# A decoder step on one core: GpSimd adds the squares of the output projection's first twelve results, and TensorE sums the first half one fill sooner

## The reference

```python
y = jnp.einsum('bte,ed->btd', o, w_o)          # output projection
def rms_norm(x, g):
    xf = x.astype(jnp.float32)
    y = xf * lax.rsqrt(jnp.mean(xf * xf, axis=-1, keepdims=True) + EPS)
    return (y * g.astype(jnp.float32)).astype(x.dtype)
hp = hp + rms_norm(yp, g[1])
hp = hp + rms_norm(sq_relu_mlp(rms_norm(hp, g[2]), mlp_w1[i], mlp_w2[i]), g[3])
```

## Time and profile before

| | us |
|---|---|
| median of 3 runs | 1491.09 |
| their range | 1486.6 to 1492.05 |
| profiled execution | 1489.39 |
| its span in the trace | 1487.0 |
| TensorE busy | 1445.9 |
| DVE busy | 895.9 |
| ACT busy | 421.9 |
| GpSimd busy | 354.4 |

### The profile page before, as it was taken

How to read it: one execution, slowest core, us unless ns; L and a number is a source line. 1 busy time by engine, 2 the same in 40 slices (tenths; PEclk the granted TensorE clock), 3 DMA queues, 4 the chain that set the end, 5 groups by cost and what they waited for, 6 DMA issues and landing times. The chain is left out here.

```text
span 1487.0 us, 25888 instructions
## 1 busy us (share of the span) xinstructions
PE 1445.9 (97%) x9729; PEld 1206.7 (81%) x9729; DVE 895.9 (60%) x1957; ACT 421.9 (28%) x1065; POOL 354.4 (24%) x463
## 2 busy tenths in 40 slices
PE   8999999999999899999999999999999999999998
PEld 7877999655557788888888889688888888888888
DVE  2755444888454985664767735666585556776513
ACT  3011343888421533334200002443431111000012
POOL 0000300477340379990320033370000000000000
PEclk9999999999999999999999999999999999999999
DMA  8346670411685624464344321712313131322201
GB/s 276 106 137 152 191 210 28 129 51 58 211 293 115 240 100 161 139 221 167 116 130 129 100 65 52 289 49 80 109 57 113 58 113 57 113 85 86 85 29 58
DMA packets 144429, 184.34 MB, mean 124 GB/s; under 512 B 31298, under 2 KB 103690, under 8 KB 143282
## 3 DMA queue, kind: packets, MB, share of 16 engines
q1 hardware_dynamic: 141938, 176.41, 36.5%
q0 software_dynamic: 2368, 6.30, 1.2%
HBM read 163.42 MB, written 29.69 MB: 130 GB/s over the span
## 5 line engine op out<-in xcount | busy, mean ns | idle before, releaser
L2842 POOL TENSOR_SCALAR att_p<-att_p,att_tot,gates 128x128 f32<-128x128 f32 (+3 forms) x128 | 79.1, 631 | 45.5 <-DVE att_tot L2764 44.8
L1062 PE MATMUL psum<-l_up_t,l_w_sums 128*128 128x260 f32 x336 | 78.2, 382 | 0.0
L1062 PE MATMUL psum<-xT,l_w 128*128 128x260 f32 x320 | 74.0, 383 | 1.6 <-PEq L113 1.6
L305 PE MATMUL psum<-xT,l_w 128*128 128x260 f32 x320 | 72.6, 388 | 1.8 <-PEq L113 1.8
L2364 PE MATMUL psum<-cmp_xt,cmp_w 64*128 64x256 f32 (+1 forms) x640 | 72.2, 362 | 0.3 <-DVE cmp_xt L2285 0.3
L1062 PEld LDWEIGHTS psum<-l_up_t,l_w_sums 128*128 128x128 f32 x336 | 63.8, 190 | 9.8
L305 PEld LDWEIGHTS psum<-xT,l_w 128*128 128x128 f32 x320 | 61.8, 194 | 11.9 <-issue 2.2
L2815 ACT ACTIVATE att_p<-att_p,att_low 128x128 f32<-128x128 f32 (+3 forms) x128 | 70.4, 554 | 3.1 <-DVE att_low L2755 3.1
L1062 PEld LDWEIGHTS psum<-xT,l_w 128*128 128x128 f32 x320 | 60.7, 190 | 11.1 <-issue 1.8
L1356 ACT ACTIVATE l_hidden<-l_tmp 128x260 f32<-128x260 f32 x64 | 26.4, 420 | 146.8 <-DVE l_tmp L1576 146.8
L2755 DVE CUSTOM_DVE_ANT_0 att_p<-psum,causal 128x128 f32<-128x128 f32 (+3 forms) x128 | 55.8, 487 | 18.9 <-PE psum L2587 17.9
(11 more groups left out here) (628 smaller groups left out, 3200.8 us busy)
## 6 DMA issues: line engine op xcount, KB each, us to landing
l_w<-in_mlp_w SPq DMA_DIRECT2D x16, 2048.0 KB, 7.7
l_w<-in_mlp_w SPq DMA_DIRECT2D x32, 1024.0 KB, 5.3
sa_rows<-in_cache_kv_sel SPq DMA_DIRECT2D x68, 128.0 KB, 2.5
proj_w<-in_nsa_w_in SPq DMA_DIRECT2D x4, 2048.0 KB, 10.1
cmp_raw<-in_cache_kv_cmp SPq DMA_DIRECT2D x24, 256.0 KB, 3.0
xT<-in_cache_kv_cmp SPq DMA_DIRECT2D x24, 256.0 KB, 3.0
hT<-in_cache_kv_cmp SPq DMA_DIRECT2D x16, 256.0 KB, 3.1
l_w<-in_nsa_w_o SPq DMA_DIRECT2D x2, 2048.0 KB, 13.0
```

Source lines behind the costliest of these rows:

```text
L305: mm = nc.tensor.matmul(ps[:, n % 8, 0:HALF], w[s][:, k, m * P:(m + 1) * P], src[:, kk, cols(h)], start=(kk == 0), stop=(kk == last))
L1062: mm = nc.tensor.matmul(ps[:, bank, 0:HALF], left(k), right(k), start=(fresh and k == 0), stop=(ends and k == KC - 1))
L2842: ve.tensor_scalar(pr[:, n % PR, par, at:at + w], pr[:, n % PR, par, at:at + w], tot[:, n % PR, u, par:par + 1], c.gates[:, i, gate:gate + ...
```

## The change

- TensorE: `sum_squares("mix", 0, 12)` stands behind fill 12 (`m == 0`) and no longer behind fill 13.
- ACT: the root of half 0 stands ahead of the copy and the square of fill 13.
- DVE: the powers run without a break; additions 0 to 11 are gone. Left are 12, ahead of the reciprocal of half 0, and 13, behind it, and 14 and 15 as before.
- GpSimd: `add_squares`, called by `tables.pool` behind the diagonal and ahead of the skip rows, does additions 0 to 11, each when its square is there, and waits until the twelfth is complete.

```diff
 @block.tensor
-                    if h == 1 and m == 1:
+                    if h == 1 and m == 0:
                         sum_squares("mix", 0, A_FILLS - 4)
 @block.scalar
-            for n in range(10, 14):
+            for n in range(10, 13):
                 keep_mix(n)
             root("mix", 0)
+            keep_mix(13)
             feed("mix", 0, 0, 3)
 @block.vector
-            def add_group(i):
-                for n in range(4 * i, 4 * i + 4):
-                    add_mix(n)
-
-            tables.dve_powers(dve, add_group)
-            for n in range(8, 14):
-                add_mix(n)
+            tables.dve_powers(dve)
+            add_mix(12)
             dve.wait_ge(c.h_back, 16)
             inverse("mix", 0)
+            add_mix(13)
             join("mix", 0, 0, 5)
 @block.gpsimd
+            def add_squares():
+                for n in range(A_FILLS - 4):
+                    h = n % 8 // 4
+                    pool.wait_ge(squared["mix"], n + 1)
+                    if n in (0, 4):
+                        nc.gpsimd.tensor_copy(acc[:, h], sq[:, n % 2]).then_inc(added["mix"], 1)
+                    else:
+                        pool.wait_ge(added["mix"], n)
+                        nc.gpsimd.tensor_add(acc[:, h], acc[:, h], sq[:, n % 2]).then_inc(added["mix"], 1)
+                pool.wait_ge(added["mix"], A_FILLS - 4)
 def pool(...)
             link(ve.tensor_copy(self.diag[at], c.ident[at, at]))
+        begin()
         pool.wait_ge(self.d_loaded, 16 * 4)
 def dve_powers(...)
-        between(0)
...
-        between(1)
```

More of the change, by code:

```diff
@@ L898, in _ @@
         def _(pool):
-            tables.pool(pool, lambda eng: eng.wait_ge(x_ready, 2 * KD), lambda eng: eng.wait_ge(up_done, 7 * PAIRS),
+            def add_squares():
[8 more added lines that the diff above has]
+                pool.wait_ge(added["mix"], A_FILLS - 4)
+            tables.pool(pool, add_squares, lambda eng: eng.wait_ge(x_ready, 2 * KD), lambda eng: eng.wait_ge(up_done, 7 * PAIRS),
                         lambda eng: eng.wait_ge(step_done, 7 * STEPS))
@@ L3591, in dve_k, with dve_powers @@
         ins.then_inc(self.k_kept, 1)
-    def dve_powers(self, dve, between):
+    def dve_powers(self, dve):
         c, ve = self.c, self.c.nc.vector
@@ L3685, in dve_powers, with pool @@
         dve.sem_inc(self.pw_ready, 1)
-    def pool(self, pool, mix_done, up_done, down_done):
+    def pool(self, pool, begin, mix_done, up_done, down_done):
         c, ve = self.c, self.c.nc.gpsimd
```

## The result

The changed kernel takes 1492.41 us (median of 20 runs, 1490.32 to 1496.14), the kernel before 1489.65 (20 runs beside them, 1486.6 to 1494.59): ratio 1.002, 95% interval 1.0012 to 1.0029. The change costs 2.8 us, by the interval 1.8 to 4.3. It was to bring 0.8.

The account below looks back on a forecast made before the run. TensorE, busy 97%, was taken as the bound, so only its waits or clock could count. 1489.39 us less 0.8 gave 1488.6; with the run median 1.7 above that execution, 1490.3 us, range 1485.5 to 1493.5.

Parts of the forecast that it names:

- GpSimd's additions: Additions 0 to 11 on GpSimd: 0.70 us each, 0.78 from start to start, the twelfth done at 494.0 us.
- The first wait goes: TensorE before the first sum of squares: its 3.46 us stall disappears, as the twelfth addition ends before fill 12.
- rival 3: DVE's joins of the first half: GpSimd's pushed-back chain ends too late, addition 15 at 515.6, time 1494.3 us; chance 0.22.
- One join per operation of GpSimd, at 1.1 to 1.4 us: DVE's joins beside GpSimd's b_bar products: one gets through per GpSimd operation, 1.1 to 1.4 us each, then 0.40 to 0.48.
- Rival 1: DVE's joins: two DVE operations per operation of GpSimd, gain 3.2 us, time 1487.9 us; chance 0.16.
- rival 2: DVE's joins: no hindrance by GpSimd, the full gain of 7.5 us, time 1483.6 us; chance 0.08.
- GpSimd's chain ends: GpSimd's 13.3 us of work queued behind the additions, up to the six products and sums, ends at about 507.4 us.
- The second sum: TensorE's second sum of squares starts at 513.3 us instead of 514.13, a gain of 0.8 us.
- One idle of 5.2 us instead of 5.84 in two: TensorE waits once, from 508.1 to 513.3 us before the second sum, instead of before both sums.
- Clock. "I take the same, so nothing in the sum": TensorE's low clock after the idle: costs the same 1.65 us as before, so adds 0 to the sum.
- twice as long (loss 1.7): Upper bound on the clock term: the low-clock stretch behind TensorE's idle doubles, a loss of 1.7 us.
- Nothing else changes behind the stage: TensorE behind the second sum: no new waits, since what it reads from DVE and ACT moves by the same amount.

Follow-up runs that it names:

- changed again: The changed kernel run once more, unaltered, for a second profile: 1494.58 us, ratio 1.0035 to the kernel before.
- padded: The changed kernel with 12 clears of 128x32 added on DVE behind the powers: 1493.15 us, ratio 1.0022 to the kernel before.
- sum moved alone: Kernel before with only the sum, root and addition 13 moved, DVE still doing all additions: 1491.57 us, ratio 1.0019.
- GpSimd adds alone: Only the additions moved to GpSimd; sum, root and addition 13 in the places of the kernel before: 1492.88 us, ratio 1.0022.
- again: The kernel before, unchanged but for one empty line ahead, timed once more: 1489.88 us, ratio 1.0003.
- with 12 more on GpSimd: The kernel before with 12 clears of 128x16 added on GpSimd where it waits for a DMA: 1489.13 us, ratio 0.9998.
- before, with both late edits: Kernel before with GpSimd's b_bar products behind the last x and TensorE's tables' products one or two pairs later: 1489.31 us, ratio 0.9995.
- the kernel kept busy: The changed kernel with 12 useless TensorE products ahead of the second sum: 1488.18 us, ratio 0.9994 to the kernel before.

## Why the prediction was wrong

Point by point:

- *GpSimd's additions*: 0.70 us taken, 0.73 measured; from start to start 0.78 taken, 0.88 measured for the seven in a row (6.00 us). The difference is idle time: 0.14 us before each, where the forecast took the 0.08 between two products of b_bar. Ahead of each addition the trace has a semaphore record of its own (L903, the wait for the addition before); between those products it has none. The 0.88 is the same beside DVE's last powers as behind them (from 492.8 on DVE is idle), so DVE is not the reason; it is DVE's small operations that take 0.62 us there instead of 0.19. The twelfth was complete at S + 32.9; predicted S + 32.35. In time for the sum: right.
- *The first wait goes*: right. *The root sooner*: ready at 499.51, S + 36.2 (predicted 497.8, which is the same S + 36.2).
- *Addition 12 beside L3715*: 2.03 us; the forecast gave it no price but named it in rival 3. It ended 0.3 us behind the root and made the reciprocal start 0.2 us behind it.
- *One join per operation of GpSimd, at 1.1 to 1.4 us*: right, 1.28, or 1.49 where GpSimd's own operation took 1.33. Rival 1 (two per operation) and rival 2 (no hindrance) fell.
- *GpSimd's chain ends* at 509.80, S + 46.5; predicted 507.4, S + 45.8. *The second sum* at S + 51.96; predicted S + 51.65. A schedule gain of 0.5 us for 0.8. Rival 3's chain never got late enough.
- *One idle of 5.2 us instead of 5.84 in two*: 5.70, in one piece: right.
- ***Clock. "I take the same, so nothing in the sum"***: this is the step that failed. The text had counted the idle's length and not its shape. One idle of 4.70 to 6.97 us was followed by 6.8 us of half clock in all five profiles that had one (changed, changed again, padded, sum moved alone, and GpSimd adds alone, which also stood 1.36 us shortly before), 2.4 to 2.9 us lost where it stands behind the second sum (2.7 in the mean of the changed kernel's three). The two shorter idles of the kernel before were followed by 3.4 us in all three profiles (before, again, and with 12 more on GpSimd), and in two of the three that stretch fell between the two sums, where the second wait took it up: 0, 0 and 1.7 lost, 0.6 in the mean. Waits of 0.44 and 2.70 us (before, with both late edits) also brought 3.4 us, and lost 1.7. The step should have read about +2.2 (0.8 to 2.9). The bound given, "twice as long (loss 1.7)", held the size of the profiled pair (1.1) and not that of the runs, since the 1.65 us of the earlier trace rows was itself the dear case of the kernel before. That the clock did it, and not the wait itself, is shown by the kernel kept busy: same second sum, the up projection 2.8 us sooner, and 3.9 us less in all.
- *Nothing else changes behind the stage*: also wrong, by 0.9 us in all seven profiles of kernels with GpSimd's additions; the cause is open.

Sum for the runs: -0.5 + 2.2 + 0.9 = 2.6 us; measured 2.8. (In the mean of three profiles of each, the second sum comes only 0.3 us sooner and the up projection 1.9 us later; with the 0.9 that is 2.8.) The predicted time, 1490.3, was built on a median of three runs that was 1.4 us above that of twenty (1491.09 to 1489.65), which hid part of the error: 1492.41 still fell within the range.

## What to carry to other kernels

Two short waits of the busiest engine are not the same as one long one of the same sum: price the granted clock behind each, and take it from several profiles, since one profile shows one draw. A stall that is gathered in one place can be filled with useless work as a test (and as a cheap cure: 2.8 us by the profiles here, 3.9 by the ratios). When a chain is pushed back, look for the next reader of its last result with the least time to spare; moving the chain paid only when that reader (the tables, 1.3 us to spare) was moved with it, and the change itself only together with both.

## What the runs showed of the hardware

- DVE and GpSimd beside one another take turns by whole instructions, but not always one for one. An addition of 128x260 on DVE: 0.43 us alone, 0.68 in the tail of one operation of GpSimd, 2.03 beside the four of L3715 (5.14 us), where it lasted beyond the ends of two of them (498.27 and 499.50), as the 3.13 us of the earlier trace rows (484.71 to 487.84) lasted beyond the ends of L3702 and of two L3708. GpSimd's own six took 1.12 to 1.34 us each meanwhile, beside the joins, and 1.06 to 1.34 before, beside the additions. The reciprocal, with one input, is 1.76 us beside GpSimd at 499.71 and 1.78 at 517.06 without it. The Trainium skill, SBUF — State Buffer, section "SBUF: two separate sides", calls the shared ports "an exclusive lock, not a bandwidth split"; these rows agree, in that an operation of DVE is held until one of GpSimd ends.
- What the half clock behind an idle costs is partly chance. The Trainium skill, TensorE: Matmul & The Clock Gate, Part 1, says of the slow products at a kernel's start that their number differs from run to run of one kernel; here the same holds in the middle: one program, with the same first wait (3.46 us), got its half clock at 514.40 us in one profile and at 504.8 in another.
- Waits of 0.36 and 0.44 us appeared some 500 us behind the edit, in code that is the same; one of them moved to another place when DVE had 12 more instructions.
